# Shift tiles ahead of the Fourier outputs, square adds on GpSimd, and a row-by-row start of the first FFN

## What is computed

```python
sh1, sc1, gt1, sh2, sc2, gt2 = ada_params(c, w_mod, b_mod)   # silu(c) @ w_mod + b_mod, split in six
a = modulate(x, g_norm_mix, sh1, sc1)                        # rms_norm(x, g) * (1 + scale) + shift
y = fourier_mix(a, w_fnet_out)      # real part of an FFT over tokens and over 4 groups of 256 features, @ w_out
h = x + gt1 * y
h = h + gt2 * conv_ffn(modulate(h, g_norm_ffn, sh2, sc2), w_ffn_up, w_ffn_conv, b_ffn_conv, w_ffn_down)
```

## Time and profile before

| | |
|---|---|
| median of 3 runs | 1581.09 us (1581.03 to 1581.62) |
| the profiled execution: device time | 1580.36 us |
| its span, first to last instruction | 1578.6 us |
| busy: PE / POOL / DVE / ACT | 98% / 64% / 50% / 20% |
| mean granted TensorE clock | 0.992 |
| DMA | 172.45 MB, mean 109 GB/s |
| chain that ended last | PE 90%, DVE 2%, POOL 1% |

### The profile page before, as it was taken

One profiled execution on the slowest core, in us unless ns is written; L12 is line 12 of the kernel. 1 busy time (PEld: TensorE's weight loads), 2 busy tenths in 40 slices (PEclk: granted clock), 3 DMA queues, 4 the chain that ended last, 5 costly groups with the idle time before them and its releaser, 6 DMA issues.

```text
span 1578.6 us, 19522 instructions
## 1 busy us (share of the span) xinstructions
PE 1550.5 (98%) x7072; PEld 1290.1 (82%) x7072; DVE 781.6 (50%) x872; ACT 308.6 (20%) x481; POOL 1003.2 (64%) x790
## 2 busy tenths in 40 slices
PE   7999999999999999999999999999999999999996
PEld 6898888887887888888888888888888888888885
DVE  6885555556407655434143654556477434343014
ACT  6422111110102001112031222222322111111011
POOL 4644666667666666766647466575467667666664
PEclk9999999999999999999999999999999999999998
DMA  9881333332332333333323232233233333333331
GB/s 372 342 289 54 103 95 93 94 105 84 104 106 86 102 93 94 99 102 89 105 67 99 74 94 80 78 93 88 71 93 94 93 95 102 96 93 96 104 93 54
DMA packets 217975, 172.45 MB, mean 109 GB/s; under 512 B 5200, under 2 KB 191824, under 8 KB 217936
## 3 DMA queue, kind: packets, MB, share of 16 engines
q1 hardware_dynamic: 217936, 171.91, 34.9%
HBM read 169.80 MB, written 2.10 MB: 109 GB/s over the span
## 4 chain that ended last, share of the span: by engine, by line
PE 90%; DVE 2%; POOL 1%; ACT 0%; issue 0%; DVEq 0%; ACTq 0%; POOLq 0%
PE ps L554 30%; PE ps L557 30%; PE ps L558 30%; POOL w_lo L532 0%; DVE act_lo L1314 0%; DVE tmp L1320 0%; DVE gates L1661 0%; DVE act_lo L1419 0%; POOL w_hi L530 0%; DVE tmp L1415 0%; PE ps L851 0%; DVE res L1647 0%; DVE res L1442 0%; PE ps L670 0%; DVE tmp L1642 0%
## 5 line engine op out<-in xcount | busy, mean ns | idle before, releaser
L532 POOL TENSOR_TENSOR w_lo<-raw,w_hi 128x1024 fp32r<-128x1024 f32 x248 | 622.3, 2509 | 20.7
L554 PE MATMUL ps<-act_hi,w_hi 128*128 128x512 f32 (+1 forms) x1304 | 509.4, 391 | 3.7 <-DVE act_lo L1419 3.2
L557 PE MATMUL ps<-act_hi,w_lo 128*128 128x512 f32 (+1 forms) x1304 | 504.7, 387 | 0.0
L558 PE MATMUL ps<-act_lo,w_hi 128*128 128x512 f32 (+1 forms) x1304 | 504.7, 387 | 0.0
L529 POOL TENSOR_TENSOR w_hi<-raw,zero 128x1 fp32r<-128x1 f32 x248 | 56.4, 228 | 498.1 <-PE ps L554 498.1
L554 PEld LDWEIGHTS ps<-act_hi,w_hi 128*128 128x128 f32 x1304 | 246.9, 189 | 57.1 <-issue 4.2
L557 PEld LDWEIGHTS ps<-act_hi,w_lo 128*128 128x128 f32 x1304 | 247.1, 190 | 49.8 <-issue 1.4
L558 PEld LDWEIGHTS ps<-act_lo,w_hi 128*128 128x128 f32 x1304 | 247.0, 189 | 48.9
L530 POOL TENSOR_SCALAR w_hi<-raw 128x1023 fp32r<-128x1023 f32 x248 | 269.4, 1086 | 0.0
L554 PE MATMUL ps<-wide_hi,w_hi 128*128 128x512 f32 (+2 forms) x624 | 240.6, 386 | 2.2 <-POOL w_lo L532 1.7
L558 PE MATMUL ps<-wide_lo,w_hi 128*128 128x512 f32 (+2 forms) x624 | 239.7, 384 | 0.0
(11 more groups left out here) (193 smaller groups left out, 1458.2 us busy)
## 6 DMA issues: line engine op xcount, KB each, us to landing
raw<-in_w_in SPq DMA_DIRECT2D x88, 512.0 KB, 4.1
gates<-in_w_mod_t SPq DMA_DIRECT2D x20, 1024.0 KB, 8.2
raw<-in_w_ffn_up SPq DMA_DIRECT2D x40, 512.0 KB, 3.8
raw<-in_w_ffn_down SPq DMA_DIRECT2D x22, 512.0 KB, 3.8
raw<-in_w_ff_gate SPq DMA_DIRECT2D x22, 512.0 KB, 3.9
raw<-in_w_ff_up SPq DMA_DIRECT2D x22, 512.0 KB, 3.9
raw<-in_w_ff_down SPq DMA_DIRECT2D x22, 512.0 KB, 3.8
raw<-in_w_r_out SPq DMA_DIRECT2D x16, 512.0 KB, 3.5
```

Source lines behind the costliest of these rows:

```text
L532: nc.gpsimd.tensor_tensor(w_lo[:, two, :], raw[:, slot, :], f32(w_hi[:, two, :]), SUB).then_inc(split_done, 1)
L554: ins = mm(o, w, a, start=start, stop=False)
L557: mm(o, wl, a, start=False, stop=False)
L558: return mm(o, w, al, start=False, stop=stop)
```

## The change

Five edits. (1) DVE makes shift tiles 4, 5 and 6 between `u_lo(5)` and `f` tile 0, and tile 7 behind `f` tile 0; `shift_columns` comes after `f` tile 3 and is eight `tensor_scalar` of one column each, with two pointer scalars, in place of three linked instructions; ACT folds factor and bias into its sums. (2) `fnet_add` 1 to 6 go from DVE to POOL. (3) The hi parts of the first FFN panels go from POOL to ACT, behind squares 2 to 5; POOL's order is new. (4) `half_sums(0)` comes one tile earlier on PE; residuals 9 to 11 and their adds go into the first half's norm loop. (5) The first FFN panels are gone through row tile by row tile, the four panels inside.

```diff
@@ POOL @@
-            for m in range(1, KT):
-                fnet_lo(m)
 def first_split(p):
-                pool.wait_ge(raw_loaded[p], FNET_LOADS + 16)
-                if p < SPLIT:
-                    pool.wait_ge(fnet_done, p + 1)
-                else:
-                    pool.wait_ge(f_done, KT)
-                nc.gpsimd.tensor_scalar(hi, raw[:, p, :], 1.0, 0.0, MUL, ADD).then_inc(hi_made, 1)
                 pool.wait_ge(hi_made, p + 1)
                 nc.gpsimd.tensor_tensor(lo, raw[:, p, :], f32(hi), SUB).then_inc(split_done, 1)
-            for p in range(FIRST):
-                first_split(p)
+            def fnet_add(n):
+                t_ = FNET_TILES[n][1]
+                pool.wait_ge(res_squared[0], n + 1)
+                pool.wait_ge(squares_added[0], n - 1)
+                nc.gpsimd.tensor_tensor(tmp[:, 0, t_], tmp[:, 0, t_], tmp[:, 1, t_], ADD).then_inc(squares_added[0], 1)
+            for m in range(1, 5):
+                fnet_lo(m)
+            fnet_add(1)
+            fnet_lo(5)
+            fnet_add(2)
+            fnet_lo(6)
+            first_split(0)
+            fnet_add(3)
+            fnet_lo(7)
+            first_split(1)
+            fnet_add(4)
+            first_split(2)
+            fnet_add(5)
+            first_split(3)
+            fnet_add(6)
@@ PE @@
                 pe.wait_ge(squares_added[0], FNET_FULL - 1 + (FNET_HALF - 1) * (i + 1))
+                pe.wait_ge(res_squared[0], n)
                 mm(ps[:, bank, halves[i]], ones[:, :], tmp[:, 0, halves[i]], start=True, stop=False)
-                pe.wait_ge(res_squared[0], n)
...
-                if n == len(FNET_TILES) - 2:
+                if n == len(FNET_TILES) - 3:
                     half_sums(0, 3)
...
                     for i, t_ in enumerate(halves):
-                        for p in range(FIRST):
-                            ins = tile(ps[:, p, t_], UP[0] + p, first_weights(p), act_hi[:, :, t_], act_lo[:, :, t_],
-                                       (act_ready[0], i * KT) if p == 0 else None, again=i == 0,
-                                       between=(3, lambda: half_sums(1, 4)) if i == 0 and p == 2 else None)
-                            if i:
-                                ins.then_inc(up_done[0], 1)
+                        for b in range(KT):
+                            pe.wait_ge(act_ready[0], i * KT + b + 1)
+                            for p in range(FIRST):
+                                if i == 0 and b == 0:
+                                    pe.wait_ge(split_done, p + 1)
+                                last = i == 1 and b == KT - 1
+                                ins = product(ps[:, p, t_], *w_block(first_weights(p), b), act_hi[:, b, t_], act_lo[:, b, t_],
+                                              b == 0, b == KT - 1, opens=last and p > 0)
+                                if last:
+                                    ins.then_inc(up_done[0], 1)
+                            if i == 0 and b == KT - 2:
+                                half_sums(1, 4)
@@ ACT @@
-                do(mod_early[:, m, :], mod_early[:, m, :], ACT.Identity, accum_out=small[:, 3, m:m + 1]).then_inc(shift_summed, 1)
+                do(mod_early[:, m, :], mod_early[:, m, :], ACT.Identity, scale=float(T), bias=early_cols("b_mod", m, 1),
+                   accum_out=shift_dc[:, m:m + 1]).then_inc(shift_summed, 1)
...
             shift_sum(1)
+            shift_sum(2)
...
-                if m == 0 or m == 2:
-                    shift_sum(m // 2 + 2)
+                if m == 0:
+                    shift_sum(3)
...
+            def first_hi(p):
+                act.wait_ge(raw_loaded[p], FNET_LOADS + 16)
+                if p < SPLIT:
+                    act.wait_ge(fnet_done, p + 1)
+                else:
+                    act.wait_ge(f_done, KT)
+                hi_of(first_weights(p)[0], raw[:, p, :], hi_made)
             for n in range(FNET_FULL + FNET_HALF + 1):
                 fnet_square(n)
                 if 1 <= n <= 3:
                     fnet_hi(n + 4)
+                if 2 <= n <= 5:
+                    first_hi(n - 2)
...
@@ DVE @@
-            for m in range(4, KT):
-                u_lo(m)
+            u_lo(4)
+            u_lo(5)
+            mod_tile(0, 4)
+            u_lo(6)
+            mod_tile(0, 5)
+            u_lo(7)
+            mod_tile(0, 6)
             def shift_columns():
                 dve.wait_ge(u_made, KT)
-                link(tt(udc, f32(dc_column(wide_hi[:, S_U:S_U + KT, :])), f32(dc_column(wide_lo[:, S_U:S_U + KT, :])), ADD))
                 dve.wait_ge(shift_summed, SHIFT_POOL)
...
-                tt(udc, udc, shift_dc, ADD).then_inc(dc_step, 1)
-            mod_tile(0, SHIFT_POOL)
+                for m in range(KT):
+                    ins = ts(udc[:, m:m + 1], lo[:, m:m + 1], hi[:, m:m + 1], shift_dc[:, m:m + 1], ADD, ADD)
+                ins.then_inc(dc_step, 1)
...
-                if SHIFT_POOL + m + 1 < KT:
-                    mod_tile(0, SHIFT_POOL + m + 1)
-                if m == KT - SHIFT_POOL:
+                if m == 0:
+                    mod_tile(0, 7)
+                if m == 3:
                     shift_columns()
...
             for i, t_ in enumerate(halves):
-                if i:
-                    fnet_residual(10)
-                    fnet_add(9)
-                    fnet_residual(11)
-                    fnet_add(10)
...
+                    if i == 0 and k in (1, 3, 5):
+                        fnet_residual(9 + k // 2)
+                        fnet_add(8 + k // 2)
```

More of the change, by code:

```diff
@@ L1060, in _ @@
                     fnet_hi(n + 4)
+                if 2 <= n <= 5:
+                    first_hi(n - 2)
             for i, t_ in enumerate(halves):
                 std(0, tmp[:, 2, :], 4 if i else 3, t_, i + 1)
-                if i == 0:
-                    fnet_square(FNET_FULL + FNET_HALF + 1)
                 for k in range(KT):
@@ L1067, in _ @@
                     hi_of(act_hi[:, k, t_], tmp[:, NORMED[k % 3], t_], norm_hi_made[0], bias=mod[:, 3 * KT + k:3 * KT + k + 1])
-                if i == 0:
-                    fnet_square(FNET_FULL + FNET_HALF + 2)
-                    fnet_square(FNET_FULL + FNET_HALF + 3)
+                    if i == 0 and k in (2, 4, 6):
+                        fnet_square(FNET_FULL + FNET_HALF + k // 2)
             ffn_gate(0)
@@ L1248, in _ @@
             link(stt(out=mod_bias(1), in0=mod_bias(1), scalar=1.0, in1=early_cols("g_norm_mix", 0, KT), op0=ADD, op1=MUL))
-            link(ts(mod_bias(0), mod_bias(0), float(T), None, MUL))
+            link(ts(mod_bias(0)[:, 0:SHIFT_POOL], mod_bias(0)[:, 0:SHIFT_POOL], float(T) / D, None, MUL))
+            link(ts(mod_bias(0)[:, SHIFT_POOL:KT], mod_bias(0)[:, SHIFT_POOL:KT], float(T), None, MUL))
             x_rstds(0)
@@ L1268, in _ @@
             mod_tiles(1, range(6, 8))
-            for m in range(4, KT):
-                u_lo(m)
+            u_lo(4)
[5 more added lines that the diff above has]
+            mod_tile(0, 6)
             def shift_columns():
                 dve.wait_ge(u_made, KT)
-                link(tt(udc, f32(dc_column(wide_hi[:, S_U:S_U + KT, :])), f32(dc_column(wide_lo[:, S_U:S_U + KT, :])), ADD))
                 dve.wait_ge(shift_summed, SHIFT_POOL)
-                link(stt(out=shift_dc[:, 0:SHIFT_POOL], in0=small[:, 3, 0:SHIFT_POOL], scalar=float(T), in1=mod_bias(0)[:, 0:SHIFT_POOL],
-                         op0=MUL, op1=ADD))
                 dve.wait_ge(mod_step, mod_done(0, KT - 1))
-                tt(udc, udc, shift_dc, ADD).then_inc(dc_step, 1)
-            mod_tile(0, SHIFT_POOL)
+                hi, lo = (f32(dc_column(w[:, S_U:S_U + KT, :])) for w in (wide_hi, wide_lo))
+                for m in range(KT):
+                    ins = ts(udc[:, m:m + 1], lo[:, m:m + 1], hi[:, m:m + 1], shift_dc[:, m:m + 1], ADD, ADD)
+                ins.then_inc(dc_step, 1)
             half = T // 2
@@ L1291, in _ @@
                 nc.vector.tensor_copy(f[:, half:half + 1], even[:, half:half + 1]).then_inc(f_made, 1)
-                if SHIFT_POOL + m + 1 < KT:
-                    mod_tile(0, SHIFT_POOL + m + 1)
-                if m == KT - SHIFT_POOL:
+                if m == 0:
+                    mod_tile(0, 7)
+                if m == 3:
                     shift_columns()
-            mod_tiles(2, [0])
+            mod_tiles(2, range(2))
             dve.wait_ge(dc_step, DC_HI_MADE)
@@ L1337, in fnet_add @@
                 dve.wait_ge(squares_added[0], n - i)
-            mod_tiles(2, range(1, KT))
+            mod_tiles(2, range(2, KT))
             dve.wait_ge(mod_step, mod_done(2, KT - 1))
@@ L1347, in _ @@
             mod_tiles(4, range(0, 2))
-            fnet_add(1)
             fnet_residual(2)
             mod_tiles(4, range(2, 4))
-            fnet_add(2)
             fnet_residual(3)
             mod_tiles(4, range(4, 6))
-            fnet_add(3)
             fnet_residual(4)
@@ L1357, in _ @@
```

(5 more changed lines are left out.)

## The result

The median of 17 runs is 1583.23 us (1581.49 to 1585.63) against 1580.48 (1578.86 to 1581.62) for 17 runs of the kernel before beside them: a ratio of 1.0020, 95% interval [1.0013, 1.0026]. The change costs 2.75 us by the medians, 3.2 by the ratio (0.0020 of 1580), and the interval excludes 1. The profiled execution took 1581.92, 1.56 more than the one of before; it is one of the fastest three of its 17, where the 1580.36 of before is near the median of that kernel.

The account below looks back on a forecast made before the run. PE bounds the kernel (busy 98%): its work plus moments idle or slowed. Head -1.1, Fourier-stage stalls +3.0 and +2.5, stretch to panel 4 -3.4 gave +1.0: 1581.4, with 0.7 for the median 1582.1; range 1578.0 to 1585.0.

Parts of the forecast that it names:

- Head, edit 1: Up to the second Fourier tile: the column product starts 1.0 earlier; 1.1 us gained, bounds 0.5 to 2.5.
- Stall for Fourier panel 7: Fourier stage, eighth tile: PE waits 3.0 us for POOL's lo part, queued behind first panel 0's landing.
- Wait at the first sums: Before half_sums(0): PE waits 2.4 to 2.5 us for the last square, ready at 100.1.
- Rival B: Clock falls in the four new gaps: 1585 with one more full half-clock stretch, 1588 with two; chance 0.11.
- Gap before half 1: Between the halves of the first FFN panels: PE idles 3.1 us after the second sums.
- Gap before panel 4: Four panels finish together, so the product of pair 0 ends 3.0 us behind the last matmul; panel 4 at 136.7.
- From Fourier's end to panel 4: Last Fourier tile's end to panel 4's start: 29.8 us instead of 33.2, a gain of 3.4.
- signs of being wrong: Dense PE from 55 to 101, column product later than 49.7, or more than one 0.50 stretch behind 60 us.
- signs of being right: Among them: column product near 48.7, PE idle 3 before the eighth Fourier tile, 2 to 3 before half_sums(0).
- Rival A: Fourier-stage stalls do not come, as first panel 0's landing or ACT's order is better than read: 1576.6; chance 0.14.
- Rival D: Start goes as wanted and only the pair's stall and the gap remain small, or edits cancel: 1581; chance 0.05.
- Rival C: Column instructions wait for POOL's lo parts, so tile 7 and the column product are 1.6 late: 1583.7; chance 0.05.

Follow-up runs that it names:

- e1: Only the shift-tile part of the change (new shift-tile order, eight column instructions), on the kernel before: 1576.88 us, ratio 0.9982 to before.
- e2: Kernel after with Fourier panel 7 and the adds ahead of the first FFN panels in ACT's and POOL's queues: 1577.47 us, ratio 0.9983 to before.
- e4: Kernel after with the second sums after four row tiles of half 0 instead of seven: 1580.23 us, ratio 0.9997 to before.
- e9: e7 with the second sums after four row tiles of half 0: 1572.44 us, ratio 0.9960 to before.
- e3: Kernel after with half 1 done as panels 0 and 1 row tile by row tile, then 2 and 3: 1578.46 us, ratio 0.9989 to before.
- e7: e1 plus row order of the products, four panels in half 0, two and two in half 1, sums late: 1576.16 us, ratio 0.9982 to before.
- e6: Kernel after with the amendments of e2, e3 and e4 together: 1568.44 us, ratio 0.9937 to before.
- e11: e2 with the first FFN panels again one after the other: 1576.75 us, ratio 0.9986 to before.
- e5: Kernel after with the first FFN panels again one after the other: 1581.81 us, ratio 1.0013 to before.
- e10: e6 with shift tile 5 moved behind the last u_lo on DVE: 1569.32 us, ratio 0.9936 to before.

## Why the prediction was right, and where its terms were off

It forecast 1582.1 against 1581.09, a loss of 1.0 by a sum of gains and losses that nearly cancel; 1583.23 against 1580.48 was measured, a loss of 2.75, inside the range. The 0.7 between profiled execution and median came from three runs; by 17 it is 0.1. In the profiled execution the start of panel 4, the number that it compares, moved by +1.38 where it had +1.0, and in part this is luck: up to the start of half 0 the profile is 1.4 ahead of the text (105.5 against 106.9), behind it 1.8 slower. Step by step:

- **Head, edit 1: -1.1 predicted, -2.3 measured** (59.93 against 62.24). The column product began at 49.11 where the text had 48.7, in an execution whose first part was 1.3 later than before's (its first odd part began at 36.21 against 34.92), which no edit touches. Of the 2.3, 0.6 is the product's start and 1.7 a stretch at half clock of 3.4 us (53.7 to 57.1) in place of 6.8. The term was too small because the text let the loss of clock cancel between product and tile; it gave 2.5 as the bound if the clock didn't fall there. e1, alone, is worth near 3. How much of that edit 1 earns every time is open: in five of the eleven kernels that have it the profile shows the full 6.8.
- **Stall for Fourier panel 7: 3.0 predicted; 2.8 measured**, released by what was named, POOL's L492. First panel 0 landed at 80.4, not 81.8, but PE was 1.2 earlier too (its last matmul before began at 84.79, so it wanted the panel at 84.9, not 86.1). e2 shows the cause, the order in the queues.
- **Wait at the first sums: 2.5 predicted, 0.8 measured.** POOL's and ACT's chain from the end of lo 7 (87.56) took 11.1 to the last square, as predicted (89.0 to 100.1). PE took 10.2 from 87.70 for the tiles that I had at 8.6, because 3.4 of it ran at half clock. Wait and slow clock together are 2.5. Rival B had said this: part of the first fall is taken from the second wait.
- **Gap before half 1: 3.1 predicted, 2.8 measured.** e4 and e9 show that it is the norm chain behind the sums. **Gap before panel 4: the product of pair 0 3.0 behind the last matmul predicted, 3.3 idle measured**, released by DVE's L1417; e3 shows that it comes from finishing the panels together.
- **From Fourier's end to panel 4: 29.8 predicted, 31.6 measured** (105.5 to 137.1). The 1.8 are the half-clock stretch from 122.0 to 125.4, 1.7 lost, which has no term in the sum.

So the terms that were mis-sized are terms of the clock. The prediction says that its sum holds one half-clock stretch behind a gap, but none stands in its terms (8.6 and 11.5 are matmuls at full clock), and there were two, of 1.7 each; and in the head the part of the fall that was absent was taken as nothing. Of the prediction's signs of being wrong one came, more than one stretch of 0.50 behind 60 us, and of its signs of being right one failed, the 2 to 3 ahead of the sums. **Rival B** was right in its mechanism and wrong in its balance: the falls behind new gaps are there, but before had 13.6 us at half clock in this part and after has 10.2, and each new stretch was 3.4 long and cost 1.7, half of the 3.4 that B put at most. What B adds is in the runs: of the kernel after's 17, those with a mean granted clock of 0.993 or 0.994 took 1581.5 to 1584.1, those with 0.989 or 0.990 took 1583.9 to 1585.6, and the median clock was 0.992. Four waits leave more places for a fall than the profiled execution shows. That this makes the whole of the 1.2 between profile and median is argued, not shown: no other run was profiled. **Rival A** was wrong for the change as written; e2 is what it would have looked like. **Rival D** missed: three of the four waits came at full size. **Rival C** is refuted. The eight column instructions took 1.54 together, 0.19 each, without a gap, while POOL ran three lo parts of 3.80 beside them. The Trainium skill, "SBUF - State Buffer", section "Who interferes with whom", counts `tensor_scalar` among the instructions that can use both port pairs, if their operands meet certain conditions, and would then have it wait for a running GpSimd instruction; for this form (one element a row, two pointer scalars) the trace does not show it. They cost 1.54 instead of my 0.6, above the bound of 1.2 too, and it was hidden as said: the product began without an idle time at 49.11, 2.6 behind the columns' end. The adds on POOL were priced well (1.28 and 0.73 to 0.77 against 1.29 and 0.65).

## What to carry to other kernels

When work is moved to an engine that has slack, what counts is its place in that engine's queue: an instruction that waits for a transfer holds up whatever is behind it, and here one swap in two queues gave 5.8 us, nearly twice the 3.2 that the whole change had cost (both by ratios). Work that frees a buffer or a bank for the next stage should finish first, even where a finer interleaving feeds the engine better. And before an edit that closes one wait is dropped as worthless, ask which wait stands next in line: on top of edit 1 the row order gave nothing clear of noise with late sums (e7), and 3.5 us with early ones (e9); early sums without the row order were not run.

## What was not expected of the hardware

The granted clock's falls are worth as much as the waits and do not only follow them. The 32 one-column passes took 3.63 us at full clock in the profiles of e1, e6, e7, e9, e11 and of the kernel after, and 4.20 to 4.95 in e2, e3, e4, e5 and e10, where the clock fell to the lower level (1.2 GHz) inside the product. In e10 it fell at 50.7, and PE had had no gap over 0.6 in the 20 us ahead. Behind the product stand 3.4 us at half clock in the kernel after, e6, e7, e9 and e11, and the stretches of e2 to e5 and e10 are 6.8 long, as in the two kernels without edit 1. In e1 it did not fall there at all (1.00 from 50 to 55), with the same instructions and nearly the same start (48.59 against 48.63). Behind gaps of 2.5 to 3.6 us it fell most times and not always, at 12 of 15 in these profiles: the kernel after had no such stretch at its panel 4, where e4 had 6.8 us and e2 3.4, and e7 and e9 had none behind the gap ahead of half 0, where dense work followed. The Trainium skill, "TensorE: Matmul & The Clock Gate", Part 1, has the clock follow how busy the engine has been; the falls behind the waits agree with it, and the one in e10 came with PE shown as busy throughout.

One and the same kernel therefore scatters: e2's runs went from 1574.75 with a mean clock of 0.996 to 1581.97 with 0.988, 7 us, more than most edits here are worth. Whether fewer waits make a kernel steadier is not shown: four of e9's five runs lie within 0.12 us, but e6's five spread over 2.5, and e3's eleven, with four gaps and 13.6 us at half clock, over 1.8.
